# Head by head: three weight subtractions move from GpSimd to VectorE, after and between the LRU tiles

## What is computed

```python
z = rmsnorm(x) @ w_in                      # q, k, lru_x, v, o, gates, g_a, g_b
conv_out = causal_conv(z[:, :c0])          # 4 taps, over lru_x, q, k
lru_y = rg_lru(conv_out[:, :D_LRU])        # h[t] = a[t] * h[t-1] + u[t]
hm = mlstm(silu(q), silu(k), v, i, f)      # 4 heads of 256, matrix memory
m_y = rmsnorm(hm) * sigmoid(o)
merged = sigmoid(g_a) * (lru_y @ w_pa) + sigmoid(g_b) * (m_y @ w_pb)
x = x + merged @ w_out
x = x + hmoe(rmsnorm(x))                   # 16 experts, top-1 group, top-2 in it
```

## Time and profile before

| what | value |
|---|---|
| median of 3 runs (lowest to highest) | 1058.31 us (1058.0 to 1059.26) |
| the profiled execution | 1057.65 us |
| its span | 1055.3 us, mean granted TensorE clock 0.96 |
| TensorE busy | 958.7 us (91%) |
| VectorE busy | 665.4 us (63%) |
| ScalarE busy | 547.4 us (52%) |
| GpSimd busy | 254.2 us (24%) |
| GpSimd's subtractions of 128 x 1024 (L664) | 72, mean 2446 ns |

### The profile page before, as it was taken

The page is one execution under the profiler, slowest core; times in us unless marked ns, Lnnn a source line. Parts: engine busy times, 40 slices in busy tenths (PEclk is TensorE's granted clock), DMA queues, the critical chain, the costliest instruction groups (busy, mean ns, idle before and its releaser), DMA issues.

```text
span 1055.3 us, 16561 instructions
## 1 busy us (share of the span) xinstructions
PE 958.7 (91%) x5935; PEld 847.0 (80%) x5935; DVE 665.4 (63%) x830; ACT 547.4 (52%) x609; POOL 254.2 (24%) x178
## 2 busy tenths in 40 slices
PE   3999899999999998999999999949999999999960
PEld 2999689888978986899999987737788888888750
DVE  5495669658866973611111113389999999989727
ACT  5645534725453472333333224457778778787622
POOL 1013223412421341434334343002001010101012
PEclk9999999999999998899999999959999999999985
DMA  9452121303222120222323368149999999999725
GB/s 302 142 168 80 47 71 43 104 27 103 60 65 70 41 79 1 80 81 80 99 79 86 93 188 307 60 153 322 412 410 412 415 413 415 413 414 414 289 108 199
DMA packets 146738, 193.67 MB, mean 184 GB/s; under 512 B 14487, under 2 KB 91693, under 8 KB 146577
## 3 DMA queue, kind: packets, MB, share of 16 engines
q1 hardware_dynamic: 139000, 165.27, 45.2%
q0 software_dynamic: 4656, 16.21, 4.0%
q10 hardware_dynamic: 3048, 11.75, 2.8%
HBM read 173.43 MB, written 19.77 MB: 183 GB/s over the span
## 4 chain that ended last, share of the span: by engine, by line
PE 74%; DVE 12%; issue 7%; ACT 4%; DMA 2%; DVEq 1%; POOL 0%; POOLq 0%; ACTq 0%; SPq 0%
PE PJ L450 61%; DVE MEM_R L1884 2%; PE NM L1272 2%; PE PJ L1221 1%; DVE MEM L1646 1%; PE MS L1451 1%; PE MS L1292 1%; PE MS L1254 1%; PE NM L450 1%; DMA MEM<-in_x_prompt_dram 1%; PE NM L1399 1%; PE MS L1282 1%; DMA MEM<-expert_rows,MEM 1%; PE NM L1482 1%; DVE MEM_R L1556 1%
## 5 line engine op out<-in xcount | busy, mean ns | idle before, releaser
L450 PE MATMUL PJ<-MEM_R 128*128 128x272 f32 (+2 forms) x5016 | 804.2, 321 | 13.3 <-ACT MEM L857 4.5
L450 PEld LDWEIGHTS PJ<-MEM_R 128*128 128x128 f32 x5016 | 722.6, 190 | 77.2 <-issue 9.2
L664 POOL TENSOR_TENSOR MEM_R<-RAW,MEM_R 128x1024 fp32r<-128x1024 f32 x72 | 175.6, 2446 | 323.7 <-ACT MEM_R L798 323.6
L1884 DVE TENSOR_TENSOR MEM_R<-CHUNK,MEM_R 128x2048 fp32r<-128x2048 f32 x100 | 224.4, 2284 | 16.1 <-ACT MEM_R L1055 14.8
L1055 ACT CAST MEM_R<-CHUNK 128x2048 fp32r<-128x2048 f32 x100 | 189.3, 1911 | 14.1 <-PE PJ L450 11.4
L798 ACT CAST MEM_R<-RAW 128x1024 fp32r<-128x1024 f32 x81 | 84.5, 1051 | 124.5 <-DMA RAW<-in_w_pb_dram 35.3
L1824 DVE TENSOR_TENSOR MERGED<-PJ,MEM 128x544 f32<-128x544 f32 x16 | 11.6, 724 | 146.9 <-PE PJ L450 146.9
L747 POOL COPY MEM<-MEM 128x1 uint32 (+1 forms) x16 | 18.4, 1150 | 237.9 <-PE MS L1451 237.9
L1646 DVE SCALAR_TENSOR_TENSOR MEM<-MEM 128x548 f32<-128x548 f32 x72 | 58.9, 818 | 8.5 <-DVE MEM L1644 0.9
L1064 ACT CAST MEM_R<-MS 128x1024 fp32r<-128x1024 f32 x17 | 17.3, 1016 | 35.2 <-PE MS L1451 35.2
L855 ACT COPY MEM<-PJ 128x272 f32<-128x272 f32 x24 | 9.2, 382 | 42.6 <-PE PJ L450 42.6
(11 more groups left out here) (295 smaller groups left out, 910.1 us busy)
## 6 DMA issues: line engine op xcount, KB each, us to landing
CHUNK<-in_w_gate_dram SPq DMA_DIRECT2D x34, 1024.0 KB, 8.5
CHUNK<-in_w_up_dram SPq DMA_DIRECT2D x34, 1024.0 KB, 10.2
CHUNK<-in_w_down_dram SPq DMA_DIRECT2D x34, 1024.0 KB, 8.8
RAW<-in_w_in_dram SPq DMA_DIRECT2D x56, 512.0 KB, 3.7
expert_rows<-MEM ACTq DMA_DIRECT2D x16, 512.0 KB, 5.9
expert_rows<-MEM SPq DMA_DIRECT2D x8, 512.0 KB, 5.3
RAW<-in_w_pa_dram SPq DMA_DIRECT2D x8, 512.0 KB, 3.6
RAW<-in_w_pb_dram SPq DMA_DIRECT2D x8, 512.0 KB, 3.6
```

Source lines behind the costliest of these rows:

```text
L450: ins = pe.matmul(out, w(a), x(b), start=first and n == 0, stop=last and n == 2)
L664: tt(lo, raw[slot], hi.bitcast(F32), ALU.subtract).then_inc(lo_done, 1)
L1884: tt(moe_hl[c][1], moe_raw[c], moe_hl[c][0].bitcast(F32), ALU.subtract).then_inc(chunk_lo[c], 1)
```

## The change

In heads 1, 2 and 3 GpSimd no longer makes the low parts 10, 11 and 12. VectorE does: 10 and 11 between the two LRU tiles, 12 behind the second. Two waits are new on GpSimd (for `lo_done`, ahead of each head's group 3 and ahead of mix block 3), so that the low parts are still counted in order; VectorE waits for `lo_done` and `hi_done`.

```diff
             with pool.Fori(1, H) as hd:
+                await_step(pool, lo_done, hd * NGR + 4)
                 for g in (3, 4, 5):
                     low_group(hd, g)
                 masks(hd)
-                for g in range(6, 13):
+                for g in range(6, 10):
                     low_group(hd, g)
 
+            pool.wait_ge(lo_done, W_MIX + 3)
             low(W_MIX + 3, 3)
...
+            def next_low(hd, g):
+
+                w = hd * NGR + (1 + NGR + g)
+                await_step(dve, lo_done, w)
+                await_step(dve, hi_done, w + 1)
+                tt(hl[g][1], raw[g], hl[g][0].bitcast(F32), ALU.subtract).then_inc(lo_done, 1)
...
                 lru(hd, 0)
+                if not (isinstance(hd, int) and hd == 0):
+                    next_low(hd, 0)
+                    next_low(hd, 1)
                 lru(hd, 1)
+                if not (isinstance(hd, int) and hd == 0):
+                    next_low(hd, 2)
```

## The result

| | before | after |
|---|---|---|
| median, 20 runs each | 1058.28 us (1055.09 to 1059.83) | 1059.49 us (1057.19 to 1063.11) |
| ratio after / before, 95% interval | | 1.002, 1.0011 to 1.003 |
| the profiled execution | 1057.65 us | 1062.37 us |
| its span, mean granted TensorE clock | 1055.3 us, 0.96 | 1060.6 us, 0.959 |
| VectorE busy | 665.4 us | 654.8 us |

The change makes the kernel slower by 1.2 us in the median and by 0.11% to 0.3% by the ratio; the forecast was +1.33 us (0.13%) and 1059.6, with most of the chance on less than 0.2%, and the ratio's middle stands just at that bound.

A forecast was written before the change was run, and what follows sets the result against it. TensorE bounds the kernel, waiting for VectorE's copy at head ends. +2.26 us (heads 1 and 2) and -0.93 (head 3) give +1.33 on the median 1058.31: 1059.64 us, range 1057.3 to 1062.0.

The forecast's parts named there:

- most of the chance on less than 0.2%: Whole kernel: chance 0.70 of staying within 0.2% of before, 0.24 of slower and 0.06 of faster by more.
- The path: End of heads 1 and 2: VectorE's way to the copy outlasts TensorE's work by 0.34 us, so VectorE additions are paid.
- The third subtraction, +1.13 in heads 1 and 2: Low part 12, between last scan and copy, lengthens TensorE's idle time by 1.13 us per head, +2.26 us together.
- the row ahead of head 0: The same subtraction ahead of head 0: next VectorE operation starts 1.13 us later, taken as the price despite a listed 1.22.
- Head 3, -0.93: End of head 3: GpSimd's block 3 no longer meets the last scan; copy starts at 393.43 instead of 394.36, -0.93 us.
- equal ends: End of head 3: GpSimd's subtraction ends at 394.35 and VectorE's copy starts at 394.36, cited against the scan staying long.
- Low parts 10 and 11 and the freed tile 0, nothing: Between the LRU tiles: two added subtractions cost nothing; shortening tile 0 gains nothing, as TensorE's gate matmuls cover it.
- The first rival: TensorE's clock falls behind the 1.47 us gaps at the scores: 1061.07 us for one head, 1062.50 for both; chance 0.14.
- it allowed 1.6 us for one fall more or less: At the numerators, a low clock more or less moves any forecast by up to 1.6 us.

The follow-up runs named there:

- the second subtraction: Changed kernel plus another VectorE subtraction of 128 x 1024, writing unread scratch, behind the one ending heads 1 to 3: 1065.05 us, ratio 1.0075 to the kernel before.
- the second profiles: Both kernels profiled once more without edits: the changed kernel's execution took 1057.38 us, that of the kernel before 1055.08 us.
- the run with the third alone: Against the kernel before, only low part 12 moves to VectorE, behind LRU tile 1, with both new GpSimd waits: 1059.81 us, ratio 1.0021.
- the second comparison: Changed kernel run again without edits, 1057.8 us (11 runs), against 29 runs of the kernel before, 1058.03 us: ratio 1.0008 (0.9997 to 1.0019).
- four such waits: Kernel before, with block 3 waiting for head 3's second LRU tile and GpSimd's groups 6 and 7 for VectorE's fourth convolution in heads 1 to 3: 1050.77 us.

## Why the prediction was right

- *The path.* VectorE's way from the gate matmuls to the copy was the longer one by 0.34 us, so what is added there is paid: shown by the gaps, by the second subtraction, which lengthened them by as much again, and by TensorE's time from head 1 to head 2, 91.80 us before and 92.93 with the change.
- *The third subtraction, +1.13 in heads 1 and 2.* Measured +1.17 and +1.13, and +1.14 and +1.13 in the second profiles. The price from the row ahead of head 0, start to start, held: 1.12 us between subtraction and copy.
- *Head 3, -0.93.* Measured -0.90. That GpSimd's subtraction held the scan was argued from equal ends; it is now shown: with block 3 made to wait, and nothing else changed in the kernel before, the scan takes 0.26 us instead of 2.31 and the gap is gone. The rule cited beside it, on shared SBUF interfaces (the Trainium skill, GPSIMD Engine Reference, Specifications), agrees with that.
- *Low parts 10 and 11 and the freed tile 0, nothing.* Shown by the run with all three between the tiles and by the run with the third alone, in TensorE's timeline rather than in the time. One reading was small, at no cost: the two subtractions start 1.53 us apart and not 1.13 (196.10 and 197.63), because `next_low` waits for the count of the one ahead. The profile puts these 0.34 us down to ScalarE, but the third of three between the tiles waits as long, 0.33 us, and for VectorE's own subtraction.
- *The range and the clock.* The first rival did not happen: the scores behind 1.47 to 1.51 us of idleness ran at 1.00 in both profiles. The rule cited with it (the Trainium skill, TensorE: Matmul & The Clock Gate, "A second HAM failure mode: psum-queue depth-cycling") speaks of short idle times, often repeated. The run with the second subtraction had its falls behind single gaps of 2.6 us, and no run here shows whether those at group 2 come of repeated short ones. What the prediction held too small is how much the clock varies between executions of one kernel: it allowed 1.6 us for one fall more or less, and the changed kernel's 20 runs span 5.9 us. The agreement of the median, 1059.49 with 1059.6, is therefore partly luck: in the second comparison the changed kernel's median lay 0.2 us below that of before. The sum of the gaps, 1.40 against 1.33, is the better test.

## What to carry to other kernels

Before work moves to an engine that is "less loaded", find the one place where that engine is waited for and look on which side of it the work lands: here the third subtraction cost nothing ahead of the second LRU tile and 1.1 us per head behind it. Where two engines get in each other's way, a wait that lets the waited-for one go first can be worth more than moving the work (four such waits, 5.2 to 10.2 us here). When effects are of a us or two, compare the idle time at the place in question, not the times of two profiled executions.

## What was not expected of the hardware

- A VectorE copy of three words per partition took 4.36 us beside two GpSimd subtractions and 0.17 us without them; a scan took 2.31 and 0.26. Each ended with GpSimd's work (the scan at 394.44 us against 394.35, the copy at 161.99 against 161.96), although it is so short by itself; the copy was held through both subtractions, which follow each other closely.
- The lower clock did not follow the length of the gap alone. In heads 1 to 3 it stayed at 1.00 behind gaps up to 1.70 us and was at 0.50 behind 2.6; in head 0, behind 2.27 us, it was at 0.50 in the first profile of before, but in the run with three subtractions between the tiles and a waiting block 3 sixteen matmuls behind the same gap ran at their full pace:

```profile
114.56 3.34 PE L1257 MATMUL MS<-MEM 128*128 128x384 f32 x16 [2.28 <-DVE MEM L1700]
```

- Executions of one unchanged kernel differ by 4.7 to 6.9 us (1055.09 to 1059.83 and, in another comparison, 1052.29 to 1059.17 before; 1057.19 to 1063.11 after). The two profiles of the changed kernel differ by 5.0 us, and 3 of these lie in two projections that met the clock at 0.50 in one of them.
